# Weight rows dealt to partitions in neighbouring groups, and strided reads on TensorE to match

## The reference, cut to what matters

```python
c_act = silu(c)                                        # 1 x 1024
mod = c_act @ w_mod[layer] + b_mod[layer]              # 1024 x 6144, split in six vectors of 1024
# layer 0: retention
xn = modulate(rms_norm(h, norm_mix[0]), sh1, sc1)
h = h + g1 * retention_mixer(xn, ret_w_in, ret_w_out)  # 1024 x 6144, 2048 x 1024
# layer 1: attention over a shared compressed key/value side (mla_w_kv_a, mla_w_q_a, ...)
# both layers: mixture of 16 experts, two per token
xn = modulate(rms_norm(h, norm_ffn[layer]), sh2, sc2)
h = h + g2 * sum_e combine[e] * ((silu(xn @ w_gate[e]) * (xn @ w_up[e])) @ w_down[e])
# w_gate, w_up: 1024 x 512 each, w_down: 512 x 1024
out = rms_norm(h, final_norm)
```

## Time and profile before

| | |
|---|---|
| median of 3 executions | 961.77 us (960.29 to 965.46) |
| the profiled execution: span | 965.0 us |
| PE, PEld, DVE, ACT, POOL busy | 909.5, 488.7, 386.0, 170.3, 34.7 us |
| DMA | 308.63 MB, mean 320 GB/s |
| DMA packets | 136,294, mean 2.3 KB |

### The profile page before, as it was taken

One profiled execution on the slowest core, in us unless ns is written; L12 is line 12 of the kernel. 1 busy time (PEld: TensorE's weight loads), 2 busy tenths in 40 slices (PEclk: granted clock), 3 DMA queues, 4 the chain that ended last, 5 costly groups with the idle time before them and its releaser, 6 DMA issues.

```text
span 965.0 us, 11805 instructions
## 1 busy us (share of the span) xinstructions
PE 909.5 (94%) x4418; PEld 488.7 (51%) x4419; DVE 386.0 (40%) x806; ACT 170.3 (18%) x318; POOL 34.7 (4%) x43
## 2 busy tenths in 40 slices
PE   3899999999998899999999888998899999999996
PEld 1588544444444454554454547774544554545542
DVE  3247878778635531222331242432621222312223
ACT  2100111211102111221102131241302211112211
POOL 0021100000001000000000011201000000000000
PEclk9799999999999999999999999999999999999999
DMA  9999999999759999899999994534299899189992
GB/s 328 385 387 345 329 387 363 341 361 350 261 175 378 338 386 393 310 397 396 389 395 397 396 382 175 175 114 142 95 356 390 312 394 392 71 320 396 396 394 102
DMA packets 136294, 308.63 MB, mean 320 GB/s; under 512 B 6051, under 2 KB 8390, under 8 KB 136262
## 3 DMA queue, kind: packets, MB, share of 16 engines
q1 hardware_dynamic: 133808, 304.42, 84.8%
q10 hardware_dynamic: 2454, 3.76, 1.2%
HBM read 307.11 MB, written 1.05 MB: 319 GB/s over the span
## 4 chain that ended last, share of the span: by engine, by line
PE 78%; DVE 8%; SPq 7%; DMA 4%; issue 2%; ACT 1%; DVEq 0%
PE bank L727 11%; PE bank L714 11%; PE bank L745 11%; PE bank L587 7%; SPq L339 6%; PE bank L580 6%; PE bank L628 6%; PE bank L771 5%; PE bank L694 5%; DVE part L1217 3%; PE bank L955 3%; DMA ring<-in_ret_w_in 2%; DMA ring<-in_moe_w_up 2%; PE bank L737 1%; PE bank L910 1%
## 5 line engine op out<-in xcount | busy, mean ns | idle before, releaser
L1217 DVE SCALAR_TENSOR_TENSOR part<-ring,cpad,part 128x512 f32<-128x512 f32 x168 | 128.4, 764 | 6.0
L727 PE MATMUL bank<-ring,arena 128*64 128x256 f32 x1088 | 125.8, 384 | 3.7 <-DMA ring<-in_moe_w_up 3.7
L1427 DVE TENSOR_TENSOR arena<-bank,arena 128x256 f32<-128x256 f32 x34 | 14.4, 424 | 250.7 <-PE bank L727 250.7
L587 PE MATMUL bank<-ring,xnT 128*128 128x512 f32 x256 | 111.4, 593 | 0.0
L745 PE MATMUL bank<-ring,arena 128*64 128x512 f32 x480 | 108.9, 595 | 0.0
L714 PE MATMUL bank<-ring,arena 128*64 128x512 f32 x480 | 106.3, 595 | 0.3 <-DVE arena L1420 0.3
L727 PEld LDWEIGHTS bank<-ring,arena 128*64 128x64 f32 x1088 | 78.8, 138 | 50.5 <-issue 16.8
L587 PEld LDWEIGHTS bank<-ring,xnT 128*128 128x128 f32 x256 | 48.2, 190 | 60.5 <-issue 60.5
L694 PEld LDWEIGHTS bank<-arena,y 128*128 128x128 f32 x544 | 64.8, 196 | 12.3 <-DVE arena L1409 7.4
L694 PE MATMUL bank<-arena,y 128*128 128x128 f32 x544 | 65.3, 280 | 3.4 <-DVE arena L1409 3.4
L714 PEld LDWEIGHTS bank<-ring,arena 128*64 128x64 f32 x480 | 33.1, 137 | 62.9 <-issue 61.3
(11 more groups left out here) (238 smaller groups left out, 782.6 us busy)
## 6 DMA issues: line engine op xcount, KB each, us to landing
ring<-in_moe_w_up SPq DMA_DIRECT2D x64, 1024.0 KB, 12.0
ring<-in_moe_w_gate SPq DMA_DIRECT2D x56, 1024.0 KB, 12.6
ring<-in_moe_w_down SPq DMA_DIRECT2D x56, 1024.0 KB, 13.9
ring<-in_w_mod SPq DMA_DIRECT2D x48, 1024.0 KB, 13.4
ring<-in_ret_w_in SPq DMA_DIRECT2D x24, 1024.0 KB, 8.3
ring<-in_w_mod_kv SPq DMA_DIRECT2D x8, 1024.0 KB, 14.3
ring<-in_ret_w_out SPq DMA_DIRECT2D x8, 1024.0 KB, 9.4
arena<-in_moe_w_down SPq DMA_DIRECT2D x2, 2048.0 KB, 12.5
```

The costliest lines, as they stand in the source:

```text
L587: ins = pe.matmul(pair[tt][:], xnT[:, k, tok(tt)], w[:, k, :], start=(k == 0), stop=(k == KT - 1))
L727: ins = pe.matmul(bank[1 + f][e * 64:(e + 1) * 64, 0:256], xgT[:, k, e * 64:(e + 1) * 64], w(2 + e, k)[:, f * 256:(f + 1) * 256], start=(k ...
L1217: ins = dve.scalar_tensor_tensor(o, w[:, k, :], cpad[:, k, 0:1], o, ALU.mult, ALU.add)
```

## The change

Everything that contracts over the model width now lies as `(p k) n`: partition `p` holds rows `8p` to `8p + 7`, which are neighbours in HBM. For the experts' gate and up a half slot is then one run of 8 KB per partition; for `moe_w_down` the rows are split in two halves of 256 and each half is `(p k)` with `k` of 2, again 8 KB; for `ret_w_out` `(p k)` with `k` of 4, 8 KB per half slot. `ret_w_in` keeps 2 KB runs, since only 512 of its 6144 columns are read at a time.

To match, turned activations must hold feature `8p + k` in partition `p`, block `k`. So the transposes and the gather take every 8th element as stationary operand (`y[:, tt, k::KT]`), `turn_head` every 4th, `turn_hidden` every 2nd.

The mod blocks change shape from 1024 x 512 to half of the rows of one whole vector, 4 rows by 1024 columns in each partition (4 KB runs). `part` becomes 1024 wide. VectorE does 4 operations of width 1024 per block and not 8 of width 512. TensorE folds a vector by 8 matmuls with every 8th element. The second half of a gate's addition is put off to the next block (`gate_sum`, `gate_store`). Bias and gain rows come as rows of 1024 and are turned by 8 strided transposes; the late vectors (L654) are turned by 16 small matmuls and not 4 transposes. Three calls of `keep_warm` (1, 2 and 2 matmuls of ones) become one of 2.

```diff
@@ source / matrix (SyncE)
-                    return w[:, b * 512:(b + 1) * 512].rearrange("(k p) n -> p k n", p=P)
+                    return w[:, b * D:(b + 1) * D].rearrange("(p k) n -> p k n", p=P)[:, 4 * (n % 2):4 * (n % 2) + 4, :]
-                return w[bass.ds(pair * 2 + j % 2, 1)].rearrange("e (k p) n -> p (e k) n", p=P)
+                w = w[bass.ds(pair * 2 + j % 2, 1)]
+                if j < 4:
+                    return w.rearrange("e (p k) n -> p (e k) n", p=P)
+                return w.rearrange("e (a p k) n -> p (e a) k n", p=P, a=2)
@@ turn_y, turn_head, gather, turn_hidden (TensorE)
-                                               y[:, tt, k * P:(k + 1) * P], ident)
+                                               y[:, tt, k::KT], ident)
-                                           on[:, tt, (2 * g + j) * P:(2 * g + j + 1) * P], ident)
+                                           on[:, tt, 2 * g + j::4], ident)
-                                                y[:, tt, k * P:(k + 1) * P], pick[:, tt, :],
+                                                y[:, tt, k::KT], pick[:, tt, :],
-                                                   hid[:, (2 * f + j) * P:(2 * f + j + 1) * P], ident)
+                                                   hid[:, f * 256 + j:(f + 1) * 256:2], ident)
@@ mod_main (VectorE)
-                steps.step(dve, dve.tensor_scalar(o, w[:, 0, :], cpad[:, 0, 0:1], None, ALU.mult))
-                for k in range(1, KT):
-                    ins = dve.scalar_tensor_tensor(o, w[:, k, :], cpad[:, k, 0:1], o, ALU.mult, ALU.add)
+                for k in range(4):
+                    c = cpad[:, 4 * half + k, 0:1]
+                    if half == 0 and k == 0:
+                        ins = dve.tensor_scalar(o, w[:, k, :], c, None, ALU.mult)
+                    else:
+                        ins = dve.scalar_tensor_tensor(o, w[:, k, :], c, o, ALU.mult, ALU.add)
@@ folds and late vectors (TensorE)
-                for j in range(4):
-                    ins = pe.matmul(bank[2 + m % 2][:, j:j + 1], part[:, m % 2, j * P:(j + 1) * P],
-                                    ones[:, 0:1], start=True, stop=True)
+                for k in range(KT):
+                    ins = pe.matmul(bank[1][:, v * KT + k:v * KT + k + 1], part[:, v, k::KT],
+                                    ones[:, 0:1], start=True, stop=True)
-            for j in range(4):
-                ins = pe.transpose(bank[6][:, 64 * j:64 * j + 64], modrow[:, j * P:(j + 1) * P], ident[0:64, 0:64])
+            for k in range(KT):
+                for g in range(2):
+                    ins = pe.matmul(bank[6][64 * g:64 * g + 64, 8 * k:8 * k + 8], modrow[:, k::KT],
+                                    ident[0:64, 32 * g:32 * g + 8], start=True, stop=True)
+            gate_sum(len(MODV) - 1, 1)
```

More of the change, by code:

```diff
@@ L66, in constants @@
     return c
-MOD = [(0, b) for b in range(12)] + [(2, b) for b in range(4)] + [(1, b) for b in range(12)]
+MODV = [(0, 0), (0, 1), (0, 2), (0, 3), (0, 4), (0, 5), (2, 0), (2, 1)] + [(1, i) for i in range(6)]
 FIRST_MOD = 4
+N_MOD = 2 * len(MODV)
 MOD_COL = {0: 0, 1: 48, 2: 96}
[L73 to L78, removed]
+GATES = {(0, 2): 0, (0, 5): 1, (1, 2): 2, (1, 5): 3}
+ROWV = [v for v in MODV[FIRST_MOD // 2:] if v not in GATES]
+VECS = [(0, 3), (2, 0), (1, 0), (1, 3)]
+FOLDED = {}
+for _v, _w in enumerate(MODV):
+    for _half in range(2 if _w in GATES else 1):
+        FOLDED[(_v, _half)] = len(FOLDED) + 1
+MOD_STORED = {}
+for _v, _w in enumerate(MODV):
+    for _half in range(2 if _w in GATES else 0 if 2 * _v >= FIRST_MOD else 1):
+        MOD_STORED[(_v, _half)] = len(MOD_STORED) + 1
+FOLDED_ALL = [max(n for (w, _), n in FOLDED.items() if w == v) for v in range(len(MODV))]
+LAST_ROW = max(v for v in range(len(MODV)) if MODV[v] not in GATES)
+N_ROWS, N_LATE = 15, 5
 WIN = [0, 2, 1, 3] + [b for h in range(RH) for b in (4 + h, 8 + h)]
@@ L121, in build_kernel @@
         gate = sb("gate", [P, 4, D])
-        part = sb("part", [P, 2, 512])
+        part = sb("part", [P, 2, D])
         cst = sb("cst", [P, C_ALL])
[L124 to L127, removed]
+        rows, late = acc[0:N_ROWS, 0, :], acc[0:N_LATE, 1, :]
+        gains = sb("gains", [3, P])
+        cols = sb("cols", [P, KT, N_ROWS])
+        gcol = sb("gcol", [P, KT, N_LATE])
+        lat_gain = sb("lat_gain", [P, 3])
         cpad = sb("cpad", [P, KT, 32])
@@ L496, in mod_parts_of @@
                     pe.wait_ge(c_silu, 1)
-                elif m >= 2:
-                    pe.wait_ge(mod_sum, m - 1)
-                for k in range(KT):
[L500 to L508, removed]
-                for j in range(4):
-                    ins = pe.matmul(bank[2 + m % 2][:, j:j + 1], part[:, m % 2, j * P:(j + 1) * P],
+                for k in range(4):
+                    for n in range(2):
+                        ins = pe.matmul(bank[2 * v + n][32 * k:32 * k + 32, :], cpad[:, 4 * half + k, :],
+                                        w[:, k, n * 512:(n + 1) * 512], start=(half == 0), stop=(half == 1))
@@ L511, in mod_fold, with gate_sum @@
+                ins.then_inc(mod_parts, 1)
+            def mod_fold(v):
+                pe.wait_ge(mod_sum, 2 * v + 2)
+                for k in range(KT):
+                    ins = pe.matmul(bank[1][:, v * KT + k:v * KT + k + 1], part[:, v, k::KT],
                                     ones[:, 0:1], start=True, stop=True)
                 ins.then_inc(mod_folded, 1)
+            def gate_sum(v, n):
+                if v > FIRST_MOD // 2 or n:
+                    pe.wait_ge(mod_stored, MOD_STORED[(v, n)] - 1)
+                pe.matmul(bank[5][:], ones, part[:, v % 2, n * 512:(n + 1) * 512], start=True, stop=True).then_inc(mod_folded, 1)
@@ L514, in mod_gather @@
             def mod_gather(m):
[L516 to L528, removed]
+                v, half = divmod(m, 2)
@@ new lines, in mod_gather @@
+                if half == 0:
+                    if MODV[v - 1] in GATES and 2 * (v - 1) >= FIRST_MOD:
+                        gate_sum(v - 1, 1)
+                    return
+                pe.wait_ge(mod_sum, m + 1)
+                if MODV[v] in GATES:
+                    gate_sum(v, 0)
+                    return
+                row = ROWV.index(MODV[v])
+                at = C_ROW + P - 1 - row
+                for g in range(2):
+                    ins = pe.matmul(bank[4][32 * g:32 * g + 32, :], cst[:, at:at + 32], part[:, v % 2, g * 512:(g + 1) * 512],
+                                    start=(row == 0), stop=(v == LAST_ROW))
@@ L1199, in mod_main @@
             def mod_main(m):
+                v, half = divmod(m, 2)
                 i = AT[("mod", m)]
-                w = slot(i).rearrange("p (k n) -> p k n", k=KT)
-                o = part[:, m % 2, :]
+                w = slot(i).rearrange("p (k n) -> p k n", k=4)
+                o = part[:, v % 2, :]
                 if m < FIRST_MOD:
-                    dve.wait_ge(mod_parts, m + 1)
-                    if m >= 2:
-                        dve.wait_ge(mod_folded, m - 1)
-                    dve.tensor_copy(o, bank[m % 2][:]).then_inc(mod_sum, 1)
+                    if half:
+                        dve.wait_ge(mod_parts, m + 1)
+                        for n in range(2):
+                            dve.tensor_copy(o[:, n * 512:(n + 1) * 512], bank[2 * v + n][:]).then_inc(mod_sum, 1)
                     return
@@ L1222, in mod_store @@
[L1222 to L1233 removed]
+                if half == 0:
+                    dve.wait_ge(mod_folded, FOLDED_ALL[v - 2])
@@ new lines, in mod_main @@
+                for k in range(4):
+                    c = cpad[:, 4 * half + k, 0:1]
[3 more added lines that the diff above has]
+                        ins = dve.scalar_tensor_tensor(o, w[:, k, :], c, o, ALU.mult, ALU.add)
+                    if half == 0 or k < 3:
+                        steps.step(dve, ins)
+                if half == 0:
+                    dve.sem_inc(mod_sum, 1)
+                else:
+                    ins.then_inc(mod_sum, 1)
@@ new lines, in gate_store @@
+            def gate_store(v, n):
+                dve.wait_ge(mod_folded, FOLDED[(v, n)])
+                dve.wait_ge(gb_in, 16 * 4)
+                o = gate[:, GATES[MODV[v]], n * 512:(n + 1) * 512]
+                dve.tensor_tensor(o, bank[5][:], o, ALU.add).then_inc(mod_stored, 1)
+            def mod_store(m):
+                v, half = divmod(m, 2)
+                if half == 0:
+                    if MODV[v - 1] in GATES:
+                        gate_store(v - 1, 1)
+                elif MODV[v] in GATES:
+                    gate_store(v, 0)
@@ L1235, in _, with first_store @@
+            def first_store(v):
+                w, b = MODV[v]
+                dve.wait_ge(mod_folded, v + 1)
+                dve.tensor_tensor(modc[:, KT * b:KT * b + KT], bank[1][:, v * KT:(v + 1) * KT], cols[:, :, 1 + b],
+                                  ALU.add).then_inc(mod_stored, 1)
```

137 lines of the change are left out of this document (65 added, 72 removed).

## The result

| | before | after |
|---|---|---|
| median of 4 executions of each | 962.62 us (960.29 to 965.46) | 1029.53 us (1029.15 to 1030.26) |
| span of the profiled execution | 965.0 us | 1027.4 us |

The changed kernel is slower: ratio 1.069, 95% interval 1.0665 to 1.0719. The forecast was 1024 us. Its sum was +62 us against a span, and the spans differ by 1027.4 - 965.0 = 62.4 us; the medians differ by 1029.53 - 962.62 = 66.9 us. The two do not agree because the profiled execution before is a long one: executions of this kernel take 2.2 us more than their span, so its 965.0 stands for about 967.2 us, while the profiled execution after took 1029.21, next to its median.

The account below looks back on a forecast made before the run. PE was taken as the bound, DMA almost level. Terms of 54 + 5 + 3 + 3 + 4 - 3.7 - 3.7 summed to +62 us, giving 1024 us from the median of 961.8; range 954 to 1045.

Parts of the forecast that it names:

- A: Rival on the weight loads: strided ones run at full pace, no longer than 112 ns, giving 956 us; chance 0.26.
- B: Rival on the weight loads: a partial stride cost, say 150 ns per load, giving 982 us; chance 0.12.
- C: Rival on PE's clock: it falls in each round's gather, 60 us more, giving 1084 us; chance 0.09.
- D: Rival on the weight loads: slower than halved, up to 440 ns and 1145 us, midway 1084; chance 0.07.
- gather, 15 rounds: MoE gather on PE: strided loads at 217 ns, not 112, add 3.4 us per round, 51 us.
- gather, first of each layer: First gather per layer: already slow at clock 0.69, so each pays only 1.5 us, together 3 us.
- late vectors: Ahead of the last wout: 4 transposes become 32 instructions, some 105 ns each, +3 us.
- start: Up to retention: strided folds, 8 row transposes and one more copy, less 1.5 us in hand, +4 us.
- waits on sums: PE's waits for VectorE at L527 (1.6 us) and L520 (2.1 us) go, gaining 3.7 us.
- waits on experts' weights: Layer 0 experts: 8 KB runs shorten the transfers, so PE's 3.7 us of waits go.
- Size of the load: Strided 128-column weight load on PE: a halved rate, 2 x 0.9 ns per column, about 217 ns.
- Transposes: Slower strided loads in turn_hidden cost +5 us over 34 times, in turn_head +3 us over eight; turn_y 0.

Follow-up runs that it names:

- Experiment 5: The kernel before with only the gather's weight loads strided, every 8th element: 1025.07 us beside 962.72, ratio 1.0636.
- experiment 1: The changed kernel with its gather alone loading contiguous slices of y again: 963.14 us beside 963.38, ratio 0.9995.
- experiment 3: The changed kernel's code with rows laid out as before, so shorter runs and all weight loads contiguous: 962.04 us beside 963.38, ratio 0.9971.
- 4: The changed kernel in full, but ScalarE writes a reordered copy of y and the gather loads contiguous slices of it: 962.47 us, ratio 0.9986.
- 8: The kernel before with the combine streaming its 512 moving columns in steps of 8 elements, its weight loads unchanged: 1028.24 us (one execution).
- experiment 9: As 4, but w_mod and ret_w_in go back to (k p) n, so the start's folds and first transpose have no stride: 958.53 us, ratio 0.9943.
- experiment 2: The changed kernel with every weight load contiguous: 928.02 us in 16 rounds, not 17; 957.3 with one round added.
- 10: As experiment 9, with four matmuls of ones ahead of the first transposes of y and one fewer later: 958.43 us, ratio 0.9949.
- 11: As experiment 3, with the same added matmuls of ones at the start as 10: 960.74 us, ratio 0.9964.
- experiment 7: The kernel before with only the gather's weight loads strided, every 2nd element (8 bytes): 966.74 us beside 962.72 (one execution).
- 6: The kernel before with only the gather's weight loads strided, every 4th element (16 bytes): 1021.1 us beside 962.72 (one execution).

## Why the prediction was right, step by step

**The bottleneck and the mechanism held.** PE is reached first, its gather is paced by its weight loads, and a stride there is paid in full 17 times. Experiment 5 shows that this alone suffices, experiment 1 that nothing else is needed. Rivals A and B (full pace, 150 ns) and C (the clock) are refuted by 234 ns at granted clock 1.00. Of D, loads slower than halved, little is left: 234 is 17 above 217, and far from 328 or 440.

**The sum came out by errors of opposite sign, which is luck.** Measured from the starts of gathers in the two timelines, one execution of each:

| step | forecast | measured |
|---|---|---|
| gather, 15 rounds | +51 | 15 x (7.49 - 3.57) = +58.8 |
| gather, first of each layer | +3 | +2.5 and +3.8 = +6.2 |
| `turn_hidden` | +5 | 34 x (0.43 - 0.37) = +2 |
| `turn_head` | +3 | 8 x (0.47 - 0.43) = +0.3 |
| late vectors | +3 | 2.02 - 0.39 = +1.6 |
| start | +4 | 45.88 - 41.84 = +4.0 |
| waits on sums | -3.7 | -4.8 |
| waits on experts' weights | -3.7 | -5.8 |
| sum | +62 | +62.3 (spans: 62.4) |

The late vectors' 2.02 is 297.37 - 295.35, from their start to the next instruction's. The waits on sums are the remainder up to the first gather: it starts 326.68 - 325.53 = 1.15 us later, and 1.15 - 4.0 - 1.6 - 0.3 = -4.8; of that 3.7 are the two waits that are gone, 1.1 has no row. The first gathers are the differences of the first rounds, 33.56 - 30.98 and 33.55 - 29.69, less 0.1 for `turn_hidden`. The waits on experts' weights are what layer 0's other seven rounds lack of 7 x 4.04 = 28.3: they last 593.30 - 360.24 = 233.1 us, before 567.04 - 356.51 = 210.5, which is only 22.5 more.

Against the medians, which differ by 66.9 us, the sum is 4.9 us short. The long execution before hides that: its first gather met the low clock (5.46 us, as in experiments 3, 4, 8 and 9, where 1, 2, 10 and 11 show 3.84), and so did its second wait for `moe_w_up`. Experiment 5 tells the same: its span of 1022.9 is 57.9 us above 965.0, its median 62.4 above the other.

- *Size of the load.* "A halved rate, 2 x 0.9 ns per column" was the right model, and 217 ns is a slip in working it out: from its own rows twice 58/64 ns over 128 columns is 232 ns, and 234 was measured. With 232 the gather comes to 32 x 120 ns = 3.84 us a round and the whole sum to about +69, or 1031 us from the median of 961.8. As recorded the gather is 8 us short over 15 rounds. Steps of 4 and 8 show that the size does not go on growing.
- *"The first round of each layer starts at clock 0.69."* That was read off layer 0 and carried to layer 1. In the kernel before, the window 692 to 697 us with layer 1's first gather has clock 1.00, and the gather took 695.79 - 692.12 = 3.67 us; it pays the whole 3.8. Layer 0's, at 0.78 now and 0.69 before, hides part of it, as argued, but less.
- *Transposes.* Their price was set by the gather's pace. But a transpose streams its 128 columns in some 107 ns and its load is shorter than the gather's: the mean of L765 is 205 ns where it was 140. At +0.04 us per 4 transposes of `turn_head` and +0.06 per 2 of `turn_hidden` it is 2.3 us in all and not 8. Even with steps of 8 a transpose pays little: 8 of `turn_y` at full clock take 1.16 us (597.07) where they took 1.09 (570.81). The late vectors are matmuls and do double, from 32 ns each in experiment 2 (32 in 1.03 us) to 63, but the 105 ns of the forecast were too many. The groups by line of the changed kernel:

```profile
L765 PEld LDWEIGHTS bank<-cst,arena 128*128 128x128 f32 x68 | 10.6, 205 | 20.3 <-issue 20.3
L529 PEld LDWEIGHTS bank<-cst,part 128*128 128x128 f32 x32 | 7.8, 334 | 2.4 <-DVE part L1238 2.4
```

  A fold, whose operand is no transpose, does have 334 ns, as the gather. What these two kinds of load differ in was not tested. A mean in such a row also holds the time that a load waits behind the one before: L729, which follows the gather and has no stride, shows 142 ns in experiment 1 and 204 here (139 to 273).
- *The wait on `moe_w_up`.* The forecast put its end down to 8 KB runs. Experiment 5 has it gone with 2 KB runs, since a round of 33.2 us leaves the transfers 31.8 us; the long runs are what removes it in a kernel with a round of 29.25 to 29.38 us (4 against 3). The term was too small because a wait costs more than itself: the kernel before, timeline of PE and window,

```profile
546.85 7.09 PE L727 MATMUL bank<-ring,arena 128*64 128x256 f32 x48 [2.47 <-DMA ring<-in_moe_w_up]
```

```profile
546.80:553.90 7.10, 7.05 (x49) 5.11 (x49) 0.42 (x1) 0.00 (x0) 0.00 (x0) 0.76 1.03 410
```

  After its 2.47 us of idleness PE ran at a granted clock of 0.76, and 48 matmuls took 7.09 us that take 5.40 at full clock (the same wait in experiment 3, where the clock stayed at 1.00): 1.7 us on top of 3.7; the last 0.4 us has no row. In experiment 7 the clock stayed at full speed too, with 5.40 us after a wait of 2.25: this part of the gain depends on the execution.
- *The start.* +4.0 as forecast, but in these two executions, and not only for its reason. Experiments 1 and 4 have the changed start untouched, and retention starts at 47.7 and 48.2; experiments 5 to 8 have the old one, and it starts at 41.0, 42.0, 43.3 and 43.1. The strides of the folds are 2.4 us of the difference: the two take 3.78 and 3.96 us in experiment 1, 3.41 and 1.95 in experiment 2, which reads no stride and still starts retention at 44.3. The clock is another part, which the forecast lacks: from 28 to 46 us it is granted at 0.69 in the changed kernel and at 0.79 before, from 28 to 42 at 0.58 to 0.74 in the three kernels with the changed start and at 0.86 to 1.00 in the five with the old. L521's third sixteen take 3.66 us and the fourth, at a higher clock, 1.94; L490's four take 3.76 us, in experiment 9 2.46. Why the clock falls lower, and what it alone is worth, the runs do not show.
- *"Those waits are few."* The forecast counts 3.7 and 1.5 us and says that no other load is waited for. It leaves out the largest, that of the first mod blocks in the waits of PE before:

```profile
PE bank L501 <- DMA ring<-in_w_mod: 10.4, 2, 8.6
```

  It is 7.9 us in the changed kernel, so the first matmul of a mod block starts at 11.97 us and not at 13.50; the later start of retention shows that this was used up.
- *The DMA side.* "At least 410 GB/s" became 421 to 434. *VectorE's sums* at 1286 ns are 1309. "L520 and L527 waiting for nobody" held, but the last fold of the new start, L529, waits 1.4 us for VectorE.

The best layout in this study keeps the long runs and has no strided operand where PE repeats it: 958.5 us, 0.6% below the kernel before and, by 0.9943 / 1.0692, 7% below the change.

## What to carry to other kernels

A layout that makes transfers longer must be paid on the engine that reads it: before changing one, count how often TensorE reads the strided operand, and price each 128-column load of a float32 matmul at twice its pace where neighbouring columns lie 16 or 32 bytes apart. A transpose costs far less, 0.01 to 0.03 us more each here. Where PE is the bound, run length is worth only the waits for DMA that it removes, here 2 to 5 us of 962 against 62 lost. If long runs are wanted, pay the reordering once, in a copy by an idle engine (4 us hidden here) or on a side where the operand is read once, and not in a loop of 17 rounds.

## What the runs showed of the hardware that was not expected

- The cost of a stride in a matmul's load is a threshold between steps of 8 and 16 bytes: 118 against 229 ns per load, then 234 at 32 bytes. A moving operand of 512 columns in steps of 32 bytes takes 926 ns against 442.
- The load of a transpose is dearer by 65 ns with steps of 2 or 4 elements (140 to 205), that of a gather with steps of 4 or 8 by 132 to 138 ns (196 to 328 and 334). A step of 2 costs a gather's load nothing, though it costs a transpose's 65 ns; no run tells why. In pace a transpose pays little all the same: 4 of them with steps of 4 take 0.47 us and not 0.43.
- After a wait of 2.47 us for a transfer the granted clock of the next 7.1 us was 0.76 in the kernel before, which is a mix of the two levels, and 1.00 after one of 2.44 us in experiment 3.
- Transfers in 8 KB runs reached 421 to 434 GB/s on one core, 4 KB 403 to 412, 2 KB 384 to 391.
